# The first projection started inside the modulation loads, a quarter of the contraction at a time

## The reference

```
mod = silu(c) @ w_ada + b_ada                 # 2048 x 12288, split in six: shift, scale, gate (twice)
shift_m, scale_m, ... = split(mod, 6)
h = rms_norm(x, pre_norm_mix) * (1 + scale_m) + shift_m
q_n, k_c, ..., g_n, q_m, k_m, v_m = split(h @ w_in)   # 5632 columns, and 24 of gates g_n
```

## Time and profile before

| | us |
|---|---|
| median of 3 runs | 3575.89 (3574.18 to 3581.48) |
| profiled execution, its own time | 3579.93 |
| its span, first to last instruction | 3577.8 |
| PE busy | 3175.6 (89%) |
| DVE busy | 1757.8 (49%) |
| ACT busy | 1277.1 (36%) |
| POOL busy | 139.0 (4%) |

### The profile page before, as it was taken

One profiled execution on the slowest core, in us unless ns is written; L12 is line 12 of the kernel. 1 busy time (PEld: TensorE's weight loads), 2 busy tenths in 40 slices (PEclk: granted clock), 3 DMA queues, 4 the chain that ended last, 5 costly groups with the idle time before them and its releaser, 6 DMA issues.

```text
span 3577.8 us, 49987 instructions
## 1 busy us (share of the span) xinstructions
PE 3175.6 (89%) x20990; PEld 2895.5 (81%) x20990; DVE 1757.8 (49%) x1499; ACT 1277.1 (36%) x1117; POOL 139.0 (4%) x105
## 2 busy tenths in 40 slices
PE   3699866989999999899976777799999899999998
PEld 3699655779888997699965666699997798889977
DVE  7655779454443444544335554234364544434444
ACT  1333122344433443333342332144333444334433
POOL 0000201000000000000003222000000000000000
PEclk6799876989999999999978887799999999999999
DMA  9777456645555555545510000255554455555553
GB/s 368 245 266 269 155 205 218 209 132 178 175 188 177 182 172 180 169 157 184 181 53 7 3 3 0 83 182 182 191 179 159 133 184 176 187 175 179 176 179 127
DMA packets 298809, 587.98 MB, mean 164 GB/s; under 512 B 11840, under 2 KB 17472, under 8 KB 298432
## 3 DMA queue, kind: packets, MB, share of 16 engines
q1 hardware_dynamic: 296176, 581.87, 49.0%
q10 hardware_dynamic: 2512, 4.36, 0.5%
HBM read 581.99 MB, written 4.19 MB: 164 GB/s over the span
## 4 chain that ended last, share of the span: by engine, by line
PE 82%; DVE 9%; ACT 3%; issue 3%; DMA 2%; POOL 0%; SPq 0%; DVEq 0%; ACTq 0%
PE ps L1687 44%; PE ps L1645 25%; PE ps L1917 3%; DMA raw<-w_ada 2%; PE ps L2074 2%; DVE ada_acc L1086 1%; DVE wL L941 1%; ACT wH L568 1%; PE ps L1961 1%; PE ps L1950 1%; DVE sq L1039 0%; PE ps L1713 0%; PE ps L1952 0%; PE ps L1738 0%; PE ps L1967 0%
## 5 line engine op out<-in xcount | busy, mean ns | idle before, releaser
L941 DVE TENSOR_TENSOR wL<-raw,wH 128x2048 fp32r<-128x2048 f32 x448 | 1026.6, 2292 | 1428.8 <-ACT wH L568 1424.0
L568 ACT ACTIVATE wH<-raw 128x2048 fp32r<-128x2048 f32 x448 | 857.4, 1914 | 1585.8 <-PE ps L1687 903.1
L1687 PE MATMUL ps<-actH,wH 128*128 128x256 f32 x4352 | 1240.5, 285 | 65.0 <-DVE wL L941 40.8
L1687 PE MATMUL ps<-actL,wH 128*128 128x256 f32 x4352 | 1238.3, 285 | 0.0
L1687 PE MATMUL ps<-actH,wL 128*128 128x256 f32 x4352 | 1237.9, 284 | 0.0
L1687 PEld LDWEIGHTS ps<-actH,wH 128*128 128x128 f32 x4352 | 842.7, 194 | 68.9 <-issue 55.1
L1687 PEld LDWEIGHTS ps<-actL,wH 128*128 128x128 f32 x4352 | 843.0, 194 | 0.0
L1687 PEld LDWEIGHTS ps<-actH,wL 128*128 128x128 f32 x4352 | 842.5, 194 | 0.0
L1645 PE MATMUL ps<-wH,hidH 128*128 128x512 f32 x1024 | 409.2, 400 | 13.0 <-ACT hid_sq L608 11.9
L1645 PE MATMUL ps<-wL,hidH 128*128 128x512 f32 x1024 | 407.6, 398 | 0.0
L1645 PE MATMUL ps<-wH,hidL 128*128 128x512 f32 x1024 | 407.6, 398 | 0.0
(11 more groups left out here) (354 smaller groups left out, 2647.0 us busy)
## 6 DMA issues: line engine op xcount, KB each, us to landing
raw<-w_in SPq DMA_DIRECT2D x96, 1024.0 KB, 5.1
raw<-w_ada SPq DMA_DIRECT2D x76, 1024.0 KB, 6.9
raw<-w_up SPq DMA_DIRECT2D x64, 1024.0 KB, 5.2
raw<-w_down SPq DMA_DIRECT2D x64, 1024.0 KB, 5.1
raw<-w_mlp_up SPq DMA_DIRECT2D x64, 1024.0 KB, 5.3
raw<-w_mlp_down SPq DMA_DIRECT2D x64, 1024.0 KB, 5.1
raw<-w_gates SPq DMA_DIRECT2D x48, 1024.0 KB, 5.2
side<-w_ada SPq DMA_DIRECT2D x20, 1024.0 KB, 7.4
```

The source lines that it names most:

```text
L568: nc.scalar.activation(wH[:, s % SPLIT if L[name]["spg"] > 1 else r % SPLIT, :, :], raw[:, slot, :, :], ACT.Copy).then_inc(wh_ready, 1)
L941: nc.vector.tensor_tensor(wL[:, b, :, :], raw[:, slot, :, :], wH[:, b, :, :].bitcast(F32), ALU.subtract).then_inc(wl_ready, 1)
L1687: ins = nc.tensor.matmul(out, w[:, b, k, cols], v[:, kk, :], start=(kk == 0 and j == 0 and n % 2 == 0), stop=(kk == STEP_K * spg - 1 and j ...
```

## The change

The eight groups of shift and scale are loaded in four pairs (a group of shift and the group of scale for the same 512 inputs). After each pair (`c`) SP loads three pieces of `w_in`: the quarter `c` of the contraction of the column groups 0, 1 and 2 (`FRONT = 3`). When the pair is there, DVE makes `mod`, `coef` and the quarter of the inputs (`front_inputs`), ACT the high part, then PE does the 48 matmuls of each of the three pieces, into six banks of the accumulator that stay open over the four quarters, and a quarter of the gates (`gate_part`). The low parts of these pieces, and that of the gates' weights, are made by GpSimd (`front_low`) instead of DVE. The loads use the same ring of four buffers, 11 of them for each `c`.

What is left of `w_in` is eight groups. Beside them six groups of modulation are done instead of five, one in each group of the loop instead of one in every two. Ten remain for later: the first attention step has one group instead of two. The gates are no longer computed behind the projection.

```diff
-SIDE = 5
+FRONT = 3
+SIDE = 6
-        ADA_BEFORE, ADA_BESIDE = (1, 1), (2, 1, 1, 1, 1, 1, 1, 1)
+        ADA_BEFORE, ADA_BESIDE = (1, 1), (1, 1, 1, 1, 1, 1, 1, 1)
+        def split_slot(name, r, s):
+            spg = L[name]["spg"]
+            return (r * spg + s) % SPLIT if spg % SPLIT else s % SPLIT
+        def front_load(c, n):
+            j = (8 + FRONT) * c + n
+            return j % RAW, 16 * (j // RAW + 1)
 # SP
-            stream("ada_a")
+            def slot_empty(c, n):
+                if n < 0:
+                    c, n = c - 1, n + 8 + FRONT
+                if c >= 0 and n < 8:
+                    sp.wait_ge(ada_sum, STEP_K * (RAW + 8 * c + n + 1))
+                elif c >= 0:
+                    sp.wait_ge(wl_ready, RAW + FRONT * c + n - 8 + 1)
+            for c in range(KT // STEP_K):
+                for n in range(8 + FRONT):
+                    slot, _ = front_load(c, n)
+                    slot_empty(c, n - RAW)
+                    k, col = (n % 4, c + 4 * (n // 4)) if n < 8 else (c, n - 8)
+                    sp.dma_start(raw[:, slot, :, :], (w_ada if n < 8 else w_in)[...]).then_inc(raw_in[slot], 16)
+                if c == 0:
+                    sp.dma_start(gw[:, :, :], matrix(a["w_gate"])).then_inc(gw_in, 16)
             sp.dma_start(c1[:, :], a["c1"]).then_inc(c1_in, 16)
-            sp.dma_start(gw[:, :, :], matrix(a["w_gate"])).then_inc(gw_in, 16)
+            sp.wait_ge(ada_rows, 2 + ADA_A)
             stream("w_in")
 # ACT
+            for c in range(KT // STEP_K):
+                inputs_high(0, 0, (c,))
+                for n in range(FRONT):
+                    split("front", 0, c, n)
+            front_out(0)
+            split("w_in", 0, 0, 0)
+            front_out(1)
+            split("w_in", 0, 0, 1)
+            front_out(2)
 # DVE
+            def front_inputs(c):
+                part = slice(GT * c, GT * (c + 1))
+                dve.wait_ge(ada_rows, 2 + 2 * (c + 1))
+                link(nc.vector.tensor_tensor(mod[:, 0:2, part], psm[:, :, part], b_ada[:, 0:2, part], ALU.add))
+                link(nc.vector.scalar_tensor_tensor(coef[:, 0, part], mod[:, 1, part], 1.0, vecs[:, 0, part], ALU.add, ALU.mult))
+                if c == 0:
+                    rstd(0)
+                for k in tiles(c):
+                    ins = nc.vector.scalar_tensor_tensor(sq[:, k, :], x_f[:, k, :], coef[:, 0, k:k + 1], std[:, :], ALU.mult, ALU.mult)
+                ins.then_inc(y_ready, 1)
+                dve.wait_ge(h_ready, c + 1)
+                for k in tiles(c):
+                    ins = nc.vector.scalar_tensor_tensor(actL[:, k, :], ...)
+                ins.then_inc(act_ready, 1)
+            for c in range(KT // STEP_K):
+                for n in range(8):
+                    ...
+                    ada_step(g, n % 4, raw[:, slot, :, :], front_acc[:, g % 2, :, :])
+                front_inputs(c)
 # GpSimd
+            def front_low(c, n):
+                slot, _ = front_load(c, 8 + n)
+                b, l = split_slot("front", c, n), lin("front", 0, c, n)
+                pool.wait_ge(wh_ready, l + 1)
+                pool.wait_ge(step_done, l + 1)
+                nc.gpsimd.tensor_tensor(wL[:, b, :, :], raw[:, slot, :, :], wH[:, b, :, :].bitcast(F32), ALU.subtract
+                                        ).then_inc(wl_ready, 1)
 # PE
+            for c in range(KT // STEP_K):
+                for h in range(2):
+                    g = 2 * c + h
+                    ada_total(g, sums=front_acc[:, g % 2, :, :], bank=6, col=c + 4 * h)
+                pe.wait_ge(act_ready, c + 1)
+                for n in range(FRONT):
+                    pe.wait_ge(wl_ready, RAW + lin("front", 0, c, n) + 1)
+                    ...   # 48 matmuls
+                    ins.then_inc(step_done, 1)
+                if c == 0:
+                    pe.wait_ge(gw_lo, 1)
+                ins = gate_part(c)   # 24 matmuls
             ins.then_inc(gate_done, 1)
+            layer("w_in", actH, actL)
```

More of the change, by code:

```diff
@@ L87, in __init__ @@
             t += n * (kind != "side")
-            if kind == "lin":
+            if kind == "front":
+                t += 8 * groups
+                lin += n
+                g += spg
+                ada += 8 * groups
+            elif kind == "lin":
                 lin += n
@@ L1050, in token_inputs @@
                         split(name, 0, 0, 1)
[L1052 to L1071, removed]
             def first_splits(name):
@@ L1702, in _ @@
                     pe.wait_ge(xT_out, n - 1)
-                tokens_out(5 + n % 2, x_f, n // (KT // GT), n % (KT // GT)).then_inc(xT_done, 1)
-            with pe.Fori(0, L["ada_a"]["groups"] // 2) as i:
-                for r in range(2):
-                    ada_total(r, i, 2)
-            layer("w_in", actH, actL, (act_ready, 0))
-            pe.wait_ge(gw_lo, 1)
-            for t in range(TT):
-                for k in range(KT):
-                    for j, (v, w) in enumerate(((actH, gwH), (actL, gwH), (actH, gwL))):
-                        ins = nc.tensor.matmul(ps[:, 5, t * GATES:(t + 1) * GATES], v[:, k, t * P:(t + 1) * P], w[:, k, :],
-                                               start=(t == 0 and k == 0 and j == 0), stop=(k == KT - 1 and j == 2),
-                                               skip_group_check=True)
+                tokens_out(5 + 2 * (n % 2), x_f, n // (KT // GT), n % (KT // GT)).then_inc(xT_done, 1)
@@ new lines, in gate_part @@
+            def gate_part(c):
+                for t in range(TT):
+                    for k in range(STEP_K * c, STEP_K * (c + 1)):
+                        for j, (v, w) in enumerate(((actH, gwH), (actL, gwH), (actH, gwL))):
+                            ins = nc.tensor.matmul(ps[:, 7, t * GATES:(t + 1) * GATES], v[:, k, t * P:(t + 1) * P], w[:, k, :],
+                                                   start=(t == 0 and k == 0 and j == 0), stop=(k == KT - 1 and j == 2),
+                                                   skip_group_check=True)
+                return ins
@@ new lines, in _ @@
+            pe.wait_ge(xT_out, 2 * (KT // GT))
+            for c in range(KT // STEP_K):
+                for h in range(2):
+                    g = 2 * c + h
+                    ada_total(g, sums=front_acc[:, g % 2, :, :], bank=6, col=c + 4 * h)
+                pe.wait_ge(act_ready, c + 1)
+                for n in range(FRONT):
+                    pe.wait_ge(wl_ready, RAW + lin("front", 0, c, n) + 1)
+                    b = split_slot("front", c, n)
+                    for k in range(STEP_K):
+                        kk = c * STEP_K + k
+                        for m in range(GT):
+                            out = ps[:, 2 * n + m // 2, (m % 2) * T:(m % 2 + 1) * T]
+                            cols = slice(m * P, (m + 1) * P)
+                            for j, (w, v) in enumerate(((wH, actH), (wH, actL), (wL, actH))):
+                                ins = nc.tensor.matmul(out, w[:, b, k, cols], v[:, kk, :], start=(kk == 0 and j == 0 and m % 2 == 0),
+                                                       stop=(kk == KT - 1 and j == 2), skip_group_check=True)
+                    ins.then_inc(step_done, 1)
+                if c == 0:
+                    pe.wait_ge(gw_lo, 1)
+                ins = gate_part(c)
```

111 lines of the change are left out of this document (57 added, 54 removed).

## The result

The changed kernel takes 3597.08 us (median of 19 executions, 3582.5 to 3601.5), beside 3578.50 for the kernel before on the same chips (19, 3569.4 to 3585.6). The ratio is 1.0048, 95% interval 1.0038 to 1.0058: 17.1 us slower, 13.6 to 20.8. The prediction was 11.9 us slower, 3588 from the median of 3575.9 known then. Of the 19 executions of each kernel the fastest are 13.1 us apart and the slowest 15.9. The profiled execution has a span of 3592.9 and a time of 3594.88.

The account below looks back on a forecast made before the run. Loads and DVE were taken to pace the modulation, then PE the projection; the change's front was bound by loads tied to GpSimd and PE. 25.8 - 5.7 - 8.2 = +11.9 us on 3575.9 gives 3588, range 3571 to 3606.

Parts of the forecast that it names:

- The tie: Front: four shared buffers make w_ada loads wait for GpSimd's w_in subtractions, which wait for PE; pairs 48.7 us apart.
- The rival without it: Front: loads run ahead and DVE sets a period of 31.2 us; time 3536, faster; chance 0.08.
- The period: Front: 48.7 us from one pair's last multiplication to the next pair's, where eight pieces alone take 21.7.
- my steps: Front: links within a pair, from column sums through rounding, subtraction and PE's step to the next pair's loads, summing to 48.7.
- The sign that I named: Front: in each period DVE idles some 10 us before a pair's fourth load, and that load ends the gap.
- my 417.0: Projection: the last step of w_in ends at 417.0 us, 25.8 later than in the kernel before.
- The clock at half in the first steps: Front: PE's first step of each pair starts at half clock and takes 8.1 us; 5.8 if the clock is up.
- The first rival: Front: same tie, but PE's clock is up in first steps and GpSimd's subtraction takes 3.8 us; 3573; chance 0.14.
- Side groups in every group of the loop: Projection: DVE's 5.0 us and two loads' 5.42 fit steps of 5.77; only six column sums of 1.68 are added.
- What comes back: Behind the projection: 5.7 us gained up to the rotary embedding from missing gates, 8.2 in attention from a missing group.
- The sum: Whole kernel: 25.8 lost in front, less 5.7 and 8.2 gained later, is 11.9 us slower.
- Dear links: Front: GpSimd and DVE take turns at each instruction and PE's clock is down; 12 to 18 us more, 3603; chance 0.18.

Follow-up runs that it names:

- e2: Changed kernel with the w_in pieces of each pair in three buffers of their own, low halves still on GpSimd; 3614.05 us, ratio 1.0089 to the kernel before.
- e3: Changed kernel with own buffers for the w_in pieces and their low halves made by DVE; 3548.41 us, ratio 0.9914 to the kernel before.
- e6: Changed kernel with 24 unused matmuls on constants ahead of each pair's first step; 3586.29 us, ratio 1.0001 to the kernel before.
- e5: Kernel before with its old front, but ten modulation groups beside the projection instead of five; 3568.21 us, ratio 0.9977.
- e10: Changed kernel as it is, executed once more; 3581.29 us.
- e9: Changed kernel with all 96 gate matmuls behind the projection again, a single execution; 3599.78 us.
- e11: Kernel before as it is, executed once more; 3571.84 us.
- e7: Changed kernel with own buffers for w_in pieces, GpSimd's low halves, and DVE waiting for GpSimd's third subtraction before the next pair's fourth piece; 3567.92 us, ratio 0.9970.
- e4: Changed kernel with ten unused matmuls on constants between each pair's column sums and first step; 3597.82 us, ratio 1.0045 to the kernel before.

## Why the prediction was right

- **The tie.** Right, down to its links. SP waits for GpSimd's third subtraction, which waits for PE's first step, and DVE waits for the loads. The rival without it was false, and so was my expectation for e2 that taking the tie away alone would gain: it lost 15 us more. It does gain once DVE has the low halves (e3).
- **The period**, 48.7. Measured 50.0 on average with the reciprocal in the first one, 49.3 by my count. From `mod` to the first use of the fourth piece my steps give 31.4; it was 32.4 (without the reciprocal), 30.2 and 32.3. From there to the last multiplication, 13.5, it was 13.6, 15.1 and 13.6: in the second pair DVE waited once more for a load. The sign that I named, a gap of DVE of some 10 us before the fourth piece, was too large: it was 4.4, 3.0 and 5.2. The first three pieces were multiplied later than I had them, since GpSimd held DVE for 4.3 us in the third (7.07 for 2.74). That lay in time in which DVE would have waited, and cost nothing. `w_in` starts 1.5 us late, which is most of the 1.9 by which its last step misses my 417.0.
- **The clock at half in the first steps.** 8.1 forecast, 8.12, 7.65, 8.61 and 7.88 measured. The first rival had the clock up; e6 shows the price of it, 8.4 us over the four steps, of the 12.7 by which `w_in` starts earlier there.
- **Side groups in every group of the loop**, costed at nothing but the column sums: steps stayed 5.77 apart, and e5 shows the same in the kernel before.
- **What comes back**, 5.7 and 8.2. Measured 5.4, and 10.1 in the profiled execution. The second term was right all the same: in e10 and in e5, where the matmuls ahead of the third step's scores are at half clock as they were before, it is 8.3. e9 confirms the first: the gates behind the projection are worth 5.7 there.
- **The sum.** +11.9 forecast, +11.7 at `w_up`'s place in the pair of profiled executions, 8.5 in e10 and e11. That the first agrees to 0.2 is luck: 1.9 more in front and 0.3 less at the rotation are made up by 10.6 between the rotation and `w_up` instead of 8.2, and 2.9 of these come from behind the third step, which I had costed at nothing. The time differs by more, +17.1 (13.6 to 20.8). My 11.9 lies outside that interval. The 5 to 9 us between lie behind all that was changed, in stages whose granted clock moves executions of either kernel by up to 15 us. In the two pairs that were profiled the difference grows there by 3.4 and 1.1. Whether the change shifts the odds of that or the executions fell so isn't settled.
- **Dear links** (turns of DVE and GpSimd at each instruction). In the changed kernel it showed as DVE held for a subtraction and cost little. In e2 it cost more than this rival had, and the other way round: the third subtraction was kept out by a run of DVE's.

The prediction said by the Trainium skill ("SBUF — State Buffer", "SBUF: two separate sides") that the two engines' common port is held for a whole instruction. The 5.12 us of two DVE multiplications beside a subtraction of 4.6 agree. That a run of 14 + 2 + 14 instructions of DVE keeps one of GpSimd out to its end (18.78, 17.50 and 17.76 us, and 5.79, 4.94 and 5.55 with one wait of DVE) is not in that rule; it is what e2 and e7 show.

## What to carry to other kernels

When two streams share one ring of buffers, the faster one runs at the pace of the slower one's last consumer: follow a buffer from its release to the next load before believing that a moved step fills idle time. Cutting such a tie can cost if it lets DVE run without a pause beside GpSimd work on the path, as in e2; give that work to DVE, or make DVE stop once for it. Where untouched stages vary by more than the change is worth, compare the places of the stages and not the time alone.

## What the hardware showed that was not expected

- GpSimd's subtraction of 128x2048 took 4.6 us, 17.5 to 18.8 beside an unbroken run of DVE's instructions, most of them with two operands in the on-chip memory, and 4.9 to 5.8 when DVE paused (e2, e7). One that came as DVE had just begun took 4.74 and held DVE instead (the kernel after).
- TensorE's clock was at half again after 5.72 us of idle time (e4) and stayed up over 0.91 and 2.10 us (e6). It also fell from 0.94 to 0.50 while PE was busy throughout with matmuls of 24 columns (e9). Executions of the same kernel differ in it: 16 matmuls in the attention took 2.7 us at full clock in one and 5.3 at half in the other.
- One untouched stage of about 810 us took 805.5 and 820.2 us in two executions of the same code. In two of the kernel before (805.4 and 818.5) the granted clock of its inner part was 0.83 and 0.80.
